# Matmuls 512 weight columns wide where tokens are stationary, in chunks of the contraction

## The reference

```python
def merge_branches(branches, gates, w_br, w_out):
    ...
    return merged @ w_out            # [512, 1024] @ [1024, 1024]

# attention:    h @ w_in[:, 512:2048]        q for 512 tokens, k and v for 768
# pool branch:  h @ w_in[:, 0:512]           512 tokens
# layer 0:      mix @ w_out_0                768 tokens, 1024 -> 1024
#               ffn(h) @ ffn_down_0          768 tokens, 2816 -> 1024
# layer 1:      att @ mla_w_o                512 tokens, 1024 -> 1024
#               ffn(h) @ ffn_down_1          512 tokens, 2816 -> 1024
```

## Time and profile before

| | |
|---|---|
| median of 3 runs | 4127.73 us (4127.23 to 4131.23) |
| span of the profiled execution | 4129.6 us |
| instructions in it | 71104 |
| TensorE matmul, busy | 3568.4 us, 86% |
| TensorE weight load, busy | 2846.9 us, 69% |
| VectorE, busy | 1697.6 us, 41% |
| ScalarE, busy | 908.8 us, 22% |

### The profile page before, as it was taken

The page is one execution under the profiler, slowest core; times in us unless marked ns, Lnnn a source line. Parts: engine busy times, 40 slices in busy tenths (PEclk is TensorE's granted clock), DMA queues, the critical chain, the costliest instruction groups (busy, mean ns, idle before and its releaser), DMA issues. The chain is left out here.

```text
span 4129.6 us, 71104 instructions
## 1 busy us (share of the span) xinstructions
PE 3568.4 (86%) x31286; PEld 2846.9 (69%) x31286; DVE 1697.6 (41%) x2906; ACT 908.8 (22%) x1502; POOL 31.9 (1%) x32
## 2 busy tenths in 40 slices
PE   5979997677997899995989976899989859979996
PEld 3858895655847655654746846888889856568886
DVE  3644544472123211113545256444452353245633
ACT  2135431041202111112011151211121212323221
POOL 0000000000000000000000000000000000000000
PEclk8979997888998899997999988999999989989998
DMA  6130004302344699993521100244422110013322
GB/s 225 57 129 4 4 4 166 123 1 94 92 143 161 253 408 410 412 412 122 174 81 56 52 2 31 65 124 115 121 75 64 43 36 25 1 52 93 97 74 80
DMA packets 274375, 483.19 MB, mean 117 GB/s; under 512 B 11947, under 2 KB 190668, under 8 KB 265397
## 3 DMA queue, kind: packets, MB, share of 16 engines
q1 hardware_dynamic: 267252, 453.97, 31.5%
q0 software_dynamic: 1728, 16.78, 1.1%
q10 hardware_dynamic: 5120, 8.39, 0.6%
HBM read 449.74 MB, written 29.36 MB: 116 GB/s over the span
## 5 line engine op out<-in xcount | busy, mean ns | idle before, releaser
L340 PE MATMUL banks<-leading,w_rest 128*128 128x512 f32 (+2 forms) x1920 | 698.9, 364 | 58.4 <-DVE w_rest L284 58.4
L340 PE MATMUL banks<-rest,w_leading 128*128 128x512 f32 (+2 forms) x1920 | 690.1, 359 | 0.0
L340 PE MATMUL banks<-leading,w_leading 128*128 128x512 f32 (+2 forms) x1920 | 688.9, 359 | 0.0
L284 DVE TENSOR_TENSOR w_rest<-land,w_leading 128x1024 fp32r<-128x1024 f32 (+2 forms) x328 | 306.9, 977 | 433.8 <-ACT w_leading L276 433.8
L276 ACT CAST w_leading<-land 128x1024 fp32r<-128x1024 f32 (+2 forms) x328 | 262.9, 849 | 875.4 <-DMA land<-in_w_in 303.0
L340 PEld LDWEIGHTS banks<-leading,w_rest 128*128 128x128 f32 (+1 forms) x1920 | 363.8, 189 | 128.8 <-DVE w_rest L284 46.0
L340 PE MATMUL banks<-w_rest,leading 128*128 128x256 f32 (+3 forms) x1332 | 394.4, 296 | 56.8 <-DVE w_rest L284 56.8
L340 PEld LDWEIGHTS banks<-leading,w_leading 128*128 128x128 f32 (+1 forms) x1920 | 364.1, 190 | 59.1
L340 PEld LDWEIGHTS banks<-rest,w_leading 128*128 128x128 f32 (+1 forms) x1920 | 364.0, 190 | 56.6
L340 PE MATMUL banks<-w_leading,rest 128*128 128x256 f32 (+3 forms) x1332 | 389.8, 293 | 0.0
L340 PE MATMUL banks<-w_leading,leading 128*128 128x256 f32 (+3 forms) x1332 | 389.4, 292 | 0.0
(11 more groups left out here) (550 smaller groups left out, 5220.5 us busy)
## 6 DMA issues: line engine op xcount, KB each, us to landing
wg<-in_w_exp_gate SPq DMA_DIRECT2D x32, 2048.0 KB, 12.7
wu<-in_w_exp_up SPq DMA_DIRECT2D x32, 2048.0 KB, 14.8
wd<-in_w_exp_down SPq DMA_DIRECT2D x32, 2048.0 KB, 11.9
ws<-in_ada_w SPq DMA_DIRECT2D x96, 512.0 KB, 3.8
land<-in_w_in SPq DMA_DIRECT2D x41, 1024.0 KB, 5.4
land<-in_ffn_up SPq DMA_DIRECT2D x44, 512.0 KB, 5.4
land<-in_ffn_up SPq DMA_DIRECT2D x88, 256.0 KB, 3.3
land<-in_ffn_down SPq DMA_DIRECT2D x24, 768.0 KB, 4.9
```

Source lines behind the costliest of these rows:

```text
L284: nc.vector.tensor_tensor(rest[s % 2][:, k0:k1, 0:n], slots[s % wslots][:, k0:k1, 0:n], leading[s % 2][:, k0:k1, 0:n].bitcast(F32), ALU.su ...
L340: mm = nc.tensor.matmul(bank_of(r, kind, at), lhsT, rhs, start=(k == 0 and q == 0), stop=(k == kt - 1 and q == len(each) - 1))
```

## The change

Every "N" product of the seven stages takes 512 weight columns per job instead of 256, with the contraction cut into chunks whose partial sums stay in PSUM, so that a step still fits the landing room. Attention: 3 jobs of 2 steps. Pool: 1 job of 2 steps, 4 banks. `w_out`, `w_out_0`, `mla_w_o`: 2 jobs of 2 steps, 8 banks. `ffn_down_0`: 2 jobs of 8 steps of 3 or 2 slices. `ffn_down_1`: 2 jobs of 6 steps of 4 or 3 slices. The chunk borders become even (`bounds`). The side pieces are spread over the visits of results (a result is visited once in each step of its job) instead of over finished results; the attention stage has 32 visits, as it had 32 results. The brought-ahead first weights take the new shapes.

```diff
-            (a["ffn_down_0"][:, 0:256], 0, -(-KF // 4), 256),
+            (a["ffn_down_0"][:, 0:512], 0, 3, 512),
...
-            ((a["ffn_up_1"][:, 0:P], a["ffn_up_1"][:, DFF:DFF + P]), 0, KD // 2, 2 * P), (a["ffn_down_1"][:, 0:256], 0, -(-KF // 4), 256)]
+            ((a["ffn_up_1"][:, 0:P], a["ffn_up_1"][:, DFF:DFF + P]), 0, KD // 2, 2 * P), (a["ffn_down_1"][:, 0:512], 0, 4, 512)]
...
-    steps = [(j, w, n, results, k0, min(k0 + size, kt)) for j, (w, n, results) in enumerate(jobs) for k0 in range(0, kt, size)]
+    bounds = [-(-kt * q // k_chunks) for q in range(k_chunks + 1)]
+    steps = [(j, w, n, results, k0, k1) for j, (w, n, results) in enumerate(jobs) for k0, k1 in zip(bounds, bounds[1:])]
...
-                return range(-(-r0 * n // total), -(-r1 * n // total))
+                return range(-(-r0 * n // ends[-1]), -(-r1 * n // ends[-1]))
...
-                        if k1 == kt:
-                            for t in sides_between(r, r + 1):
-                                side_piece(pe, t)
+                        for t in sides_between(ends[s] + i, ends[s] + i + 1):
+                            side_piece(pe, t)
...
+                        if of_visit is not None:
+                            of_visit(eng, ends[s] + i)
...
-                project_add(nc, m, a["w_out"], of_halves(pair), KD, [(t, m.x[:, t, :], gate[:, 0, :]) for t in range(NTL)], split=True, width=256)
+                project_add(nc, m, a["w_out"], of_halves(pair), KD, [(t, m.x[:, t, :], gate[:, 0, :]) for t in range(NTL)], split=True, banks=8, k_chunks=2)
...
-            jobs = [(a["w_in"][:, 512 + c:512 + c + 256], 256, [("N", t, 256) for t in range(NTC if c < 512 else 0, NT)])
-                    for c in range(0, 3 * 512, 256)]
+            jobs = [(a["w_in"][:, 512 + c:512 + c + 512], 512, [("N", t, 512) for t in range(NTC if c < 512 else 0, NT)])
+                    for c in range(0, 3 * 512, 512)]
...
-            products(nc, m, jobs, hT_of(m), evac, "vector", split=True, width=256, side=modulation_tiles(m, a, 0, 16, 48))
+            products(nc, m, jobs, hT_of(m), evac, "vector", banks=6, split=True, width=512, k_chunks=2, side=modulation_tiles(m, a, 0, 16, 48))
...
-        products(nc, m, [(a["w_in"][:, c:c + 256], 256, [("N", NTC + t, 256) for t in range(NTL)]) for c in (0, 256)], hT_of(m), evac, "scalar",
-                 split=True, width=256)
+        products(nc, m, [(a["w_in"][:, 0:512], 512, [("N", NTC + t, 512) for t in range(NTL)])], hT_of(m), evac, "scalar",
+                 split=True, width=512, k_chunks=2)
...
-                    project_add(nc, m, a["ffn_down_1"], of_halves(m.fT, first), KF, adds(c1, 5), width=256, split=True, banks=8, k_chunks=4)
+                    project_add(nc, m, a["ffn_down_1"], of_halves(m.fT, first), KF, adds(c1, 5), split=True, banks=8, k_chunks=6)
...
-                    project_add(nc, m, a["ffn_down_0"], of_halves((leading, rest)), KF, tiles, width=256, split=True, banks=8, k_chunks=4, whole=(m.fT, leading, rest))
+                    project_add(nc, m, a["ffn_down_0"], of_halves((leading, rest)), KF, tiles, split=True, banks=8, k_chunks=8, whole=(m.fT, leading, rest))
```

More of the change, by code:

```diff
@@ L146, in first_weights @@
     w_in, w_0 = a["w_in"], a["w_in_0"]
-    return [(w_in[:, 2048:2048 + 256], 0, KD, 256), (w_in[:, 512:768], 0, KD, 256), (w_in[:, 0:256], 0, KD, 256),
-            (w_in[:, 3968:3968 + 256], 0, KD, 256), (a["w_out"][:, 0:256], 0, KD, 256),
-            (w_0[:, 0:256], 0, KD, 256), (w_0[:, 1536:1792], 0, KD, 256), (w_0[:, 2560:2816], 0, KD, 256), (a["w_out_0"][:, 0:256], 0, KD, 256),
+    return [(w_in[:, 2048:2048 + 256], 0, KD, 256), (w_in[:, 512:1024], 0, KD // 2, 512), (w_in[:, 0:512], 0, KD // 2, 512),
+            (w_in[:, 3968:3968 + 256], 0, KD, 256), (a["w_out"][:, 0:512], 0, KD // 2, 512),
+            (w_0[:, 0:256], 0, KD, 256), (w_0[:, 1536:1792], 0, KD, 256), (w_0[:, 2560:2816], 0, KD, 256), (a["w_out_0"][:, 0:512], 0, KD // 2, 512),
             ((a["ffn_up_0"][:, 0:P], a["ffn_up_0"][:, DFF:DFF + P]), 0, KD, 2 * P),
-            (a["ffn_down_0"][:, 0:256], 0, -(-KF // 4), 256),
+            (a["ffn_down_0"][:, 0:512], 0, 3, 512),
             (a["mla_w_down"][:, 0:384], 0, 4, 384), (a["mla_w_uq"][:, 0:512], 0, 3, 512), (a["mla_w_ukv"][:, 0:512], 0, 2, 512),
-            (a["mla_w_o"][:, 0:256], 0, KD, 256),
-            ((a["ffn_up_1"][:, 0:P], a["ffn_up_1"][:, DFF:DFF + P]), 0, KD // 2, 2 * P), (a["ffn_down_1"][:, 0:256], 0, -(-KF // 4), 256)]
+            (a["mla_w_o"][:, 0:512], 0, KD // 2, 512),
+            ((a["ffn_up_1"][:, 0:P], a["ffn_up_1"][:, DFF:DFF + P]), 0, KD // 2, 2 * P), (a["ffn_down_1"][:, 0:512], 0, 4, 512)]
 def bring_ahead(m, sp):
@@ L186, in products @@
         ends.append(ends[-1] + len(step[3]))
-    total = sum(len(results) for w, n, results in jobs)
     with ExitStack() as ctx:
@@ L354, in side_add, with each_result @@
                 nc.vector.tensor_tensor(side[u][2], turned, bc(side[u][3].unsqueeze(2), 2), ALU.add).then_inc(side_read_sem, 1)
-            def each_result(eng, between, of_result):
+            def each_result(eng, between, of_result, of_visit=None):
                 if split:
@@ L373, in read, with sides_read @@
                 evac(bank_of(r, kind, at), j, at, chain).then_inc(read_sem, 1)
-            def read_both(dve, r, count, j, kind, at):
-                for t in sides_between(r, r + 1):
+            def sides_read(dve, visit):
+                for t in sides_between(visit, visit + 1):
                     u = t // PIECES
@@ L382, in read_both, with read_here @@
                         side_add(dve, u - 1)
+            def read_here(dve, r, count, j, kind, at):
                 if evac_on == "vector":
@@ L402, in _ @@
                     nc.vector.tensor_copy(m.cond_wide[:, :, 0:2], side[0][1]).then_inc(spread_sem, 1)
-                each_result(dve, part_weights, read_both)
+                each_result(dve, part_weights, read_here, sides_read)
                 if side:
@@ L980, in attention_branch @@
             m.q, m.k = buffers(nc, rows, q=[NTL, 512], k=[NT, 512])
-            jobs = [(a["w_in"][:, 512 + c:512 + c + 256], 256, [("N", t, 256) for t in range(NTC if c < 512 else 0, NT)])
-                    for c in range(0, 3 * 512, 256)]
+            jobs = [(a["w_in"][:, 512 + c:512 + c + 512], 512, [("N", t, 512) for t in range(NTC if c < 512 else 0, NT)])
+                    for c in range(0, 3 * 512, 512)]
             def evac(out, j, at, chain):
-                dst = (m.q, m.k, m.v)[j // 2][:, at[0] - (NTC if j < 2 else 0), 256 * (j % 2):256 * (j % 2 + 1)]
-                return nc.vector.tensor_copy(dst, out)
-            products(nc, m, jobs, hT_of(m), evac, "vector", split=True, width=256, side=modulation_tiles(m, a, 0, 16, 48))
+                return nc.vector.tensor_copy((m.q, m.k, m.v)[j][:, at[0] - (0 if j else NTC), :], out)
+            products(nc, m, jobs, hT_of(m), evac, "vector", banks=6, split=True, width=512, k_chunks=2, side=modulation_tiles(m, a, 0, 16, 48))
             head_norms(nc, m, [(m.q[:].rearrange("p t (n e) -> p (t n) e", e=HD), m.qk_gain[:, 0:HD]),
@@ L1012, in evac @@
         def evac(out, j, at, chain):
-            return nc.scalar.copy(m.u[:, at[0] - NTC, 256 * j:256 * (j + 1)], out)
-        products(nc, m, [(a["w_in"][:, c:c + 256], 256, [("N", NTC + t, 256) for t in range(NTL)]) for c in (0, 256)], hT_of(m), evac, "scalar",
-                 split=True, width=256)
+            return nc.scalar.copy(m.u[:, at[0] - NTC, :], out)
+        products(nc, m, [(a["w_in"][:, 0:512], 512, [("N", NTC + t, 512) for t in range(NTL)])], hT_of(m), evac, "scalar",
+                 split=True, width=512, k_chunks=2)
         with stage(nc, weights=1, banded=2, diffed=1, copied=1, mapped=1, read=1) as (
@@ L2201, in second_block @@
                     with halves(nc, m.mixT) as pair:
-                        project_add(nc, m, a["w_out_0"], of_halves(pair), KD, tiles, split=True, width=256)
+                        project_add(nc, m, a["w_out_0"], of_halves(pair), KD, tiles, split=True, banks=8, k_chunks=2)
                 else:
@@ L2207, in second_block @@
                     with halves(nc, m.oT) as pair:
-                        project_add(nc, m, a["mla_w_o"], of_halves(pair, CTX), KD, tiles, split=True, width=256)
+                        project_add(nc, m, a["mla_w_o"], of_halves(pair, CTX), KD, tiles, split=True, banks=8, k_chunks=2)
             with ExitStack() as c1:
```

## The result

The kernel after the change takes 4104.01 us (median of 4 runs, 4100.54 to 4105.57) against 4128.52 us for the kernel before, timed beside it: 24.5 us less, ratio 0.9936 with a 95% interval of 0.9923 to 0.9949. Timed again in five rounds it took 4103.31 us against 4129.74, ratio 0.9938 (0.9925 to 0.9952). The forecast was 4097.5 us, range 4088 to 4110, and -30.2 us. The span went from 4129.6 to 4102.9 us, and in a second profile of each kernel from 4128.3 to 4101.5.

A forecast was written before the change was run, and what follows sets the result against it. The prediction took the distance between matmul starts on TensorE as the bound. Its terms, -31.6 + 3.2 - 1.8 = -30.2 us, taken off the 4127.73 us median, gave 4097.5 us, range 4088 to 4110.

The forecast's parts named there:

- The bound: In the seven changed stages, the time is set by the distance between matmul starts on TensorE, 120.0 ns at 256 columns.
- Fewer, wider matmuls: All seven stages: 4944 matmuls become 2472, each pair 13.3 ns cheaper at full clock; -31.6 us, bounds -33 and -16.6.
- The first rival: New matmuls in the seven stages follow at 233 ns, as in layer 1's `ffn_up`; -15.2 us, 4112.5 us, chance 0.08.
- Half-clock starts: Each of the seven stages has 18 matmuls at half clock, 126 in all, on which nothing is won.
- Chunk borders: Leaving partial sums in their banks between steps costs TensorE 0, at most some 0.05 us a border.
- Can weights still be ready?: Rounding, parting and loading of the next weights stay hidden under each step; cost 0, cover 0.3 to 4 us.
- the tightest place: Last chunk in `ffn_down_1`: VectorE parts the next weights behind evictions, second half ready at 7.9 of 8.2 us.
- Evictions at the end: Behind each stage's last matmul the wider eviction is exposed: +0.54 us in five stages; +3.2 us in all, bounds +2 and +5.
- Openings: First steps' splitting and parting: -2.3 us in `ffn_down_0`, +0.5 in `ffn_down_1`; -1.8 us in all, bounds 0 and -2.4.
- late tails: Late stage ends, named with one or two stages at 233 ns as the reason for the range's high bound; no separate size.

The follow-up runs named there:

- the width kernel: Kernel before with `ffn_down_0` alone changed to 512 columns, 2 jobs of 8 steps; 4115.52 us against 4130.59, ratio 0.9958.
- the chunk kernel: Kernel before with `ffn_down_0` alone cut into 8 steps a job, still 256 columns wide; 4122.64 us in a single run.

## Why the prediction was right, and where not

*The bound* was read rightly: the distance of matmuls. No stage has a second wait for `w_rest`, and the width kernel and the chunk kernel part the effect as the prediction did.

*Fewer, wider matmuls*, -31.6 us. The distance of the earlier trace rows came out in six of seven stages (226.7 to 226.8 ns). It was right for `w_out`, `w_out_0`, `ffn_down_0` and `mla_w_o` to within 0.6 us. The step that failed is in attention. I had read from the earlier trace rows that 512 columns take 0.11 us more than 256 behind a side piece, and from that and the earlier trace rows that the fast distance holds there. The row shows only the first distance of a visit. The ten behind it have a mean of 233 ns, because a stream of 512 columns takes some distances to settle behind the side work, four at best, and behind most pieces a visit of 12 matmuls is over first. The visits of 24 narrow matmuls in before gave no warning: their distances settle too, but from 116 to 121 ns, a little under the final 120. The first rival's number turned up in one stage of seven, by another mechanism than `ffn_up`'s.

*Half-clock starts.* I took 18 matmuls at half clock per stage, and nothing won on them. The pool branch won 0.1 to 0.7 us instead of 1.0: 11 of its 96 matmuls stood at half clock, 4.7 us, where before had 12 of 192, 2.6 us. At half clock nothing is won, and the 11 wide ones hold the work of 22. That is the same effect as in layer 1, in the small. The forecast held the starts fixed; they move with every shift of a stage.

*Chunk borders*, 0: shown by the chunk kernel, in which 16 more borders leave the stretch at 191.5 us. The rule of the Trainium skill that speaks for keeping all slices of an output together ("TensorE: Matmul & The Clock Gate", section "Loop structure matters more than you think") did not bite, since the next weights were always ready.

*Can weights still be ready?* Yes, and the tightest place was read rightly. In `ffn_down_1` the last chunk of the first job runs from 4002.83 to 4010.99 us, and VectorE parts the next weights behind two evictions:

```profile
4007.11 0.69 DVE L1823 TENSOR_TENSOR t<-banks,gate_rows 128x512 f32<-128x512 f32 x1 [0.62 <-PE banks L340]
4007.84 0.69 DVE L1824 TENSOR_TENSOR x_rows<-x_rows,t 128x512 f32<-128x512 f32 x1
4008.45 2.35 DVE L284 TENSOR_TENSOR w_rest<-land,w_leading 128x1024 fp32r<-128x1024 f32 x2
```

The parting ends 8.0 us into the 8.2 of the step, where the forecast had 7.9. In `ffn_down_0`'s last chunk VectorE evicts without a pause, one result each 1.36 us, as fast as TensorE makes them (kernel after, VectorE):

```profile
3234.14 0.69 DVE L1823 TENSOR_TENSOR t<-banks,gate_rows 128x512 f32<-128x512 f32 x1
3234.87 0.69 DVE L1824 TENSOR_TENSOR x_rows<-x_rows,t 128x512 f32<-128x512 f32 x1
3235.50 0.69 DVE L1823 TENSOR_TENSOR t<-banks,gate_rows 128x512 f32<-128x512 f32 x1
```

*Evictions at the end*, +3.2 us: the pair takes 0.72 + 0.69 = 1.41 us against the 1.42 of the sum, so +0.5 us a stage (`w_out_0`, kernel after, answers to the earlier trace rows):

```profile
2604.54 0.69 DVE L1823 TENSOR_TENSOR t<-banks,gate_rows 128x512 f32<-128x512 f32 x1 [1.30 <-PE banks L340]
2605.26 0.69 DVE L1824 TENSOR_TENSOR x_rows<-x_rows,t 128x512 f32<-128x512 f32 x1
```

*Openings*, -1.8 us: -2.3 in `ffn_down_0` as said. In `ffn_down_1` the time from the last `gate_rows` copy to the first matmul went from 3.38 (3965.79 to 3969.17) to 3.86 us (3944.29 to 3948.15), the +0.5 of the sum. That stage won 5.3 instead of 5.9 us; some 0.4 of it is its start again, 13 wide distances at half clock where before had 22 narrow ones.

*What the sum left out* is the largest error: 3.8 us in layer 1, with no changed line. The terms were differences within the changed stages, and the rest was taken to stand still. The stretch between `w_out` and `w_out_0` was 1.8 to 2.0 us shorter in both pairs, but it scatters by more than that. So the mechanism of the forecast held, and its range held partly by luck: its upper end was meant for stages at 233 ns and late tails, and what used it up were starts at half clock and scatter.

## What to carry to other kernels

Where every matmul loads a new stationary operand, look up the distance between starts at two widths in the same trace: if it is columns plus a constant, halving the number of matmuls wins the constant, and the before trace may already hold a stage of the wanted width to price it. Check that price in a stage with the same interruptions too, over a whole visit and not only its first distance, since behind one a stream can take more than ten matmuls to settle. And when stages move, let the range have several microseconds for stages that you don't touch: how much of them runs at half clock depends on when they begin. It can repeat exactly from run to run, as in layer 1, and so look like an effect of the code; profile both kernels twice to tell it from what scatters.

## What the runs showed of the hardware that I had not expected

The distance of back-to-back matmuls of one shape at full clock is not one number. At 512 columns the uninterrupted streams of kind N settle at 226.7 ns, and so do some of kind T; others of kind T keep a repeating pattern, with means of 233.3 (232, 235 in `ffn_up`), 234.1 (first rwkv projections) or, after a shift of 32 bytes, 229.2 (231, 226, 229 in hyena's). The shift moved it in some stages and not in others.

Behind an interruption a stream needs some matmuls to come to its distance: at 512 columns four behind an 8-column matmul, and behind most side pieces in attention more than the ten of a visit; at 256 columns eight, which are faster than those that follow.

128 columns have the same distance at half clock as 256, 0.213 us. That stage shows TensorE busy for 448 of 448 us at a granted clock of 0.50, though the stage ahead of it ran at 1.00: 448 us against 129 for the same product.

Half clock at the openings of unchanged code can differ between two kernels and repeat within each to 0.01 us (327.74 and 327.73, 331.50 and 331.50), while another stretch of the same kernel differs by 3.4 us from one execution to the next.
